# Local attention heads: values as the stationary operand, transposed results, probabilities divided by GpSimd before they are transposed

## The reference, cut to what matters

```python
def swa_sinks_attention(q, k, v, sinks):
    ...
    scores = jnp.einsum('bnqkgd,bnskd->bnkgqs', qb, kb).astype(jnp.float32) * scale
    ...
    sink = sinks.astype(jnp.float32).reshape(1, 1, A_KV_HEADS, A_GROUP, 1, 1)
    m = jnp.maximum(jnp.max(scores, axis=-1, keepdims=True), sink)
    p = jnp.exp(scores - m)
    denom = jnp.sum(p, axis=-1, keepdims=True) + jnp.exp(sink - m)
    p = (p / denom).astype(v.dtype)
    out = jnp.einsum('bnkgqs,bnskd->bnqkgd', p, vb)
...
        mixed = jnp.concatenate([out_a.reshape(b, s, A_Q_W), out_b.reshape(b, s, B_W)], axis=-1)
        x = x + jnp.einsum('bse,ed->bsd', mixed, w_out)
```

## Time and profile before

| what | us |
|---|---|
| median of 3 runs | 2722.82 (2721.86 to 2727.66) |
| the profiled execution | 2724.15 |
| its span in the trace | 2722.3 |
| TensorE busy | 2633.6 (97%) |
| VectorE busy | 1837.4 (67%) |
| ScalarE busy | 1326.2 (49%) |
| GpSimd busy | 405.3 (15%) |
| attention stage, from its first score to the last result | 1742.2 to 1987.6 of the span |

### The profile page before, as it was taken

One profiled execution on the slowest core, in us unless ns is written; L12 is line 12 of the kernel. 1 busy time (PEld: TensorE's weight loads), 2 busy tenths in 40 slices (PEclk: granted clock), 3 DMA queues, 4 the chain that ended last, 5 costly groups with the idle time before them and its releaser, 6 DMA issues. The chain is left out here.

```text
span 2722.3 us, 37072 instructions
## 1 busy us (share of the span) xinstructions
PE 2633.6 (97%) x13612; PEld 2193.7 (81%) x13612; DVE 1837.4 (67%) x2469; ACT 1326.2 (49%) x1952; POOL 405.3 (15%) x359
## 2 busy tenths in 40 slices
PE   8999999999999899999999999899999999999999
PEld 7888876877788888888888788778888788888887
DVE  5761365457524888888888857566625875857878
ACT  3111243567432577877787422555533553525353
POOL 0222212100230122222221022300020000000000
PEclk9999999999999999999999999999999999999999
DMA  3115124311452699999999332100032616253451
GB/s 128 54 47 182 40 74 131 127 39 52 137 179 109 237 378 380 386 381 371 374 371 348 139 105 68 39 1 1 1 132 66 266 49 248 71 187 135 157 183 62
DMA packets 142456, 437.83 MB, mean 161 GB/s; under 512 B 23408, under 2 KB 45680, under 8 KB 110576
## 3 DMA queue, kind: packets, MB, share of 16 engines
q1 hardware_dynamic: 125312, 402.40, 41.0%
q0 software_dynamic: 10656, 20.99, 2.2%
q10 hardware_dynamic: 6352, 12.58, 1.2%
HBM read 387.68 MB, written 66.06 MB: 167 GB/s over the span
## 5 line engine op out<-in xcount | busy, mean ns | idle before, releaser
L2729 DVE TENSOR_TENSOR w_lo<-w_raw,w_hi 128x2048 fp32r<-128x2048 f32 x192 | 437.2, 2293 | 60.3 <-ACT w_hi L2663 59.3
L2663 ACT ACTIVATE w_hi<-w_raw 128x2048 fp32r<-128x2048 f32 x187 | 355.8, 1925 | 39.5 <-PE banks L2790 39.5
L3660 PE MATMUL banks<-b_parts,a_parts 128*128 128x512 f32 x1344 | 306.9, 390 | 6.3 <-DVE a_parts L3715 6.3
L3660 PE MATMUL banks<-a_parts,b_parts 128*128 128x512 f32 x1344 | 306.0, 389 | 2.3 <-DVE a_parts L3715 1.2
L3660 PEld LDWEIGHTS banks<-b_parts,a_parts 128*128 128x128 f32 x1344 | 251.8, 188 | 60.9 <-DVE a_parts L3715 8.8
L3660 PEld LDWEIGHTS banks<-a_parts,b_parts 128*128 128x128 f32 x1344 | 252.0, 188 | 55.2 <-DVE a_parts L3715 1.6
L3689 ACT ACTIVATE b_parts<-w_quarter 128x1024 fp32r<-128x1024 f32 x112 | 118.6, 1059 | 281.4 <-PE banks L3660 266.8
L766 POOL TENSOR_TENSOR w_lo<-w_raw,w_hi 128x512 fp32r<-128x512 f32 (+2 forms) x132 | 158.6, 1207 | 576.6 <-ACT w_hi L745 575.4
L745 ACT ACTIVATE w_hi<-w_raw 128x512 fp32r<-128x512 f32 (+2 forms) x132 | 73.9, 573 | 324.0 <-PE banks L824 306.0
L3709 DVE TENSOR_TENSOR b_parts<-w_quarter,b_parts 128x1024 fp32r<-128x1024 f32 x112 | 136.9, 1222 | 132.5 <-ACT b_parts L3689 132.5
L824 PE MATMUL banks<-w_hi,act_hi 128*128 128x512 f32 (+1 forms) x576 | 219.9, 382 | 6.0 <-POOL w_lo L766 3.7
(11 more groups left out here) (545 smaller groups left out, 5560.8 us busy)
## 6 DMA issues: line engine op xcount, KB each, us to landing
w_raw<-in_w SPq DMA_DIRECT2D x192, 1024.0 KB, 7.4
a_parts<-scratch_x_parts SPq DMA_DIRECT2D x42, 1024.0 KB, 4.8
w_raw<-in_w_in SPq DMA_DIRECT2D x80, 256.0 KB, 2.7
w_quarter<-in_w_up SPq DMA_DIRECT2D x16, 1024.0 KB, 6.9
w_quarter<-in_w_down SPq DMA_DIRECT2D x16, 1024.0 KB, 8.0
scratch_x_parts<-a_parts SPq DMA_DIRECT2D x14, 1024.0 KB, 5.1
scratch_gateT<-gate_staged SPq DMA_DIRECT2D x32, 256.0 KB, 2.2
gate<-scratch_gateT SPq DMA_DIRECT2D x32, 256.0 KB, 3.6
```

What stands on the lines that cost most here:

```text
L2663: act.activation(hi[c % SLOTS][:, :], raw[c % TILES][:, :], ACT.Copy).then_inc(hi_done, 1)
L2729: dve.tensor_tensor(lo[c % SLOTS][:, :], raw[c % TILES][:, :], hi[c % SLOTS][:, :].bitcast(F32), ALU.subtract).then_inc(lo_done, 1)
L3660: mm = pe.matmul(out, left, right, start=(start and n == 0), stop=(stop and n == 2))
```

## The change

The local units now divide first and weigh with the roles swapped.

- ScalarE makes the sinks' exponential ahead of the four others. VectorE, in iteration p+1 behind the maximum of unit p+1, waits for the exponentials of unit p and forms the inverses two heads at a time (`normalise`). GpSimd then multiplies the probabilities in place, in two instructions of two heads each. `turn(p)` waits for both.
- ScalarE makes rounded high parts of LOW and of HIGH (`a_hi`), and VectorE the low parts of both (`a_lo`). The values are split once per tile into high and low columns of one 128x128 stationary operand (`values`, `split_values`). `weigh` has four matmuls of 512 columns instead of eight float32 products. The result stands transposed in the bank, the high values' part in 64 rows and the low values' part in the other 64. ScalarE moves one part across (`cross`, two instructions), VectorE adds the other (`out`, two instructions).
- Since the local results are already transposed, the output stage transposes only the forgetting half (32 transposes). The new `MixedRows` also interleaves the rounding of weights and rows by hand-written orders, and TensorE waits per row tile (`rows_ready`) instead of for all.
- In the last tile the order of units is three forgetting, local, three forgetting, local, two forgetting.

```diff
         @block.gpsimd
         def _(pool):
-            for t in range(2, NT):
-                pool.wait_ge(scored, starts[t - 1])
-                for step in range(2):
-                    ops.pool_part(pool, t, step)
+            def normalise(p):
+                u, s, q = units[p], p % 4, probs[:, p % 3, :]
+                for a in (0, 2):
+                    pool.wait_ge(inverted, 2 * windows_upto[p] + a // 2 + 1)
+                    own, c = slice(a, a + 2), slice(a * u.keys, (a + 2) * u.keys)
+                    x = q[:, c].rearrange("p (a k) -> p a k", a=2)
+                    pool.tensor_tensor(x, x, inv[:, s, own].unsqueeze(2).broadcast_to([P, 2, u.keys]), ALU.mult).then_inc(normed, 1)
+
+            for p in range(n_units):
+                if is_window(p - 1):
+                    normalise(p - 1)
+                if prepares(p) and prepares(p)[1] < 2:
+                    pool.wait_ge(scored, starts[prepares(p)[0] - 1])
+                    pool.wait_ge(normed, 2 * windows_upto[p])
+                    ops.pool_part(pool, *prepares(p))
+                    pool.wait_ge(ops.prep_pool, ops.dve_upto[prepares(p)])
...
+            def normalise(p):
+                s = p % 4
+                for a in (0, 2):
+                    dve.wait_ge(exped, exped_upto[p] + 1 + a + 2)
+                    own = slice(a, a + 2)
+                    then(dve.tensor_tensor(inv[:, s, own], sums[:, s, own], snk[:, s, own], ALU.add))
+                    dve.reciprocal(inv[:, s, own], inv[:, s, own]).then_inc(inverted, 1)
...
             def turn(p):
                 u = units[p]
+                if u.window:
+                    pe.wait_ge(normed, 2 * windows_upto[p + 1])
+                    free_banks(p - 1)
+                    for b in range(len(u.key_tiles)):
+                        for a in range(HALF):
+                            c = a * u.keys + b * P
+                            mm = pe.transpose((LOW, HIGH)[b][:, a * P:(a + 1) * P], probs[:, p % 3, c:c + P], v.ident[:, :])
+                        mm.then_inc((turned_low, turned_high)[b], 1)
+                    return
...
+                if u.window:
+                    pe.wait_ge(values_split, u.i + 1)
+                    for b, j in enumerate(u.key_tiles):
+                        vals = values[:, j, u.g * P:(u.g + 1) * P]
+                        pe.matmul(v.bank[6 + p % 2][:, :], vals, aT_hi(p, b), start=(b == 0), stop=False)
+                        mm = pe.matmul(v.bank[6 + p % 2][:, :], vals, a_lo[:, b, :], start=False, stop=(j == u.i))
+                    mm.then_inc(weighed, 1)
+                    return
...
+class MixedRows:
+
+    BY_POOL = (3, 6)
+    ACT_ORDER = ("b0", "a0", "b1", "a1", "w0", "b2", "a2", "b3", "a3", "b4", "a4", "w1", "b5", "a5", "b6", "a6", "b7", "a7", "w2", "w3")
+    POOL_ORDER = ("w0", "a3", "w1", "a6", "w2", "w3")
```

More of the change, by code:

```diff
@@ L813, in _ @@
                         pe.wait_ge(free, freed[b])
+                    for s, count in tile.rows_ready.get(u, ()):
+                        pe.wait_ge(s, count)
                     if tile.kind == "nat":
@@ L3250, in __init__ @@
         self.width, self.exps = self.keys * (AH // AKV), AH // AKV + 1
-        first = max(0, i - 1)
-        self.blocks = [(a * self.keys + (j - first) * P, j, a, j == first, j == i) for a in range(AH // AKV) for j in range(first, i + 1)]
+        self.key_tiles = list(range(max(0, i - 1), i + 1))
 def attention2_stage(v):
@@ L3304, in attention2_stage, with is_window, aT_hi, by_side @@
     weighed, weigh_read = sem("weighed"), sem("weigh_read")
+    inverted = sem("inverted")
+    normed, values_split, hi_turned, crossed = sem("normed"), sem("values_split"), sem("hi_turned"), sem("crossed")
+    windows_upto = np.cumsum([0] + [u.window for u in units]).tolist()
+    hi_upto = np.cumsum([0] + [len(u.key_tiles) if u.window else 0 for u in units]).tolist()
+    splits_values = {0: 0, **{windows_at[t] - 1: t for t in range(1, NT)}}
+    def is_window(p):
+        return 0 <= p < n_units and units[p].window
+    def aT_hi(p, b):
+        return a_hi[:, p % 2, b * N:(b + 1) * N]
+    def by_side(x, r, side):
+        return x[r, :].rearrange("p (m e q) -> p m e q", m=2, e=2)[:, :, side, :]
+    def own_heads(u, r):
+        c = 2 * u.g * P
+        return v.out_aT[r, u.i, c:c + 2 * P].rearrange("p (m q) -> p m q", m=2)
+    SIDES = (slice(0, HD), slice(HD, P))
     def prepares(p):
@@ L3320, in turn_out, with cross @@
                     act.wait_ge(weighed, p - 1)
+                if units[p].window:
+                    for b in range(len(units[p].key_tiles)):
+                        if b:
+                            act.wait_ge(turned_high, high_upto[p + 1])
+                        act.activation(aT_hi(p, b), (LOW, HIGH)[b], ACT.Copy).then_inc(hi_turned, 1)
+                    return
                 c = min(units[p].width, N)
                 act.activation(aT[:, p % 2, :c], LOW[:, :c], ACT.Copy).then_inc(low_read, 1)
+            def cross(p):
+                u = units[p]
+                act.wait_ge(weighed, p + 1)
+                for side in range(2):
+                    act.activation(own_heads(u, SIDES[side]), by_side(v.bank[6 + p % 2], SIDES[1 - side], side), ACT.Copy).then_inc(crossed, 1)
             for p, u in enumerate(units):
@@ L3358, in turn_out @@
             def turn_out(p):
+                if units[p].window:
+                    if p >= 2:
+                        dve.wait_ge(weighed, p - 1)
+                    for b in range(len(units[p].key_tiles)):
+                        dve.wait_ge(hi_turned, hi_upto[p] + b + 1)
+                        dve.tensor_tensor(a_lo[:, b, :], (LOW, HIGH)[b], aT_hi(p, b).bitcast(F32), ALU.subtract).then_inc((low_read, high_read)[b], 1)
+                    return
                 if halves[p] < 2:
@@ L3370, in out @@
                 if u.window:
-                    then(dve.tensor_tensor(inv[:, s, :], sums[:, s, :], snk[:, s, :], ALU.add))
-                    then(dve.reciprocal(inv[:, s, :], inv[:, s, :]))
-                    c = u.g * HALF * HD
-                    dve.tensor_tensor(v.out_a[:, u.i, c:c + HALF * HD].rearrange("p (a d) -> p a d", d=HD),
-                                      v.bank[6 + p % 2].rearrange("p (a g d) -> p a g d", g=AKV, d=HD)[:, :, u.g, :],
-                                      inv[:, s, :].unsqueeze(2).broadcast_to([P, HALF, HD]), ALU.mult).then_inc(weigh_read, 1)
+                    dve.wait_ge(crossed, 2 * windows_upto[p + 1])
+                    for side in range(2):
+                        made = own_heads(u, SIDES[side])
+                        (dve.tensor_tensor(made, by_side(v.bank[6 + p % 2], SIDES[side], side), made, ALU.add)
+                         .then_inc(*((weigh_read, 1) if side else (link_a, 1))))
                 else:
@@ L3411, in _ @@
                     ops.dve_part(dve, *prepares(p), (LOW, HIGH))
[L3412 removed]
+                if p >= 3 and not is_window(p - 3):
                     out(p - 3)
+                if p in splits_values:
+                    split_values(splits_values[p])
             turn_out(n_units - 2)
@@ L3512, in output2_stage, with load_w @@
     ready, free, x_in = sem("bank_ready"), sem("bank_free"), sem("x_in")
-    prelude = turn_rows(v, mixers)
+    ring = Ring(v)
+    mixed = MixedRows(v, ring)
+    tiles[0].rows_ready = {t: mixed.row_waits(t) for t in range(NT)}
+    def load_w(sp):
+        ring.load_first(sp, tiles)
     def load_x(sp):
```

151 lines of the change are left out of this document (86 added, 65 removed).

## The result

The changed kernel takes **2737.18 us** (median of 5 runs, 2735.45 to 2739.5), the kernel before 2722.82 us (5 runs, 2721.86 to 2727.66). The ratio is 1.0049, 95% interval 1.0035 to 1.0064: slower by 14 us. The profiled execution took 2737.18 us with a span of 2735.2.

A forecast was written before the change was run, and what follows sets the result against it. TensorE, busy 2633.6 of 2722.3 us, was taken as the bound. Terms -11.7, +16.9, +5.0, +1.0, -0.3, -6.2, +4.5 summed to +9.2, from the median 2732.0, taken as 2731; own range 2727 to 2737, whole range 2716 to 2743.

The forecast's parts named there:

- Weighing: Local units in attention: four 512-column matmuls take 0.92 us instead of 1.70, saving 11.7 us in all.
- GpSimd's division: Local units in attention: TensorE's transposes wait for GpSimd's multiplications, twelve units late, +16.9 us.
- Splitting: Preparations behind local transposes: LOW and HIGH come free later through rounding and subtraction, six places, +5.0 us.
- Cover of `kb` preparations: Attention: three preparations of keys lose their cover because the weighing beside them is shorter, +1 us.
- Clock: Attention: TensorE's clock falls behind gaps of 1 to 2 us; three falls of about 1.5 us counted, +4.5 us.
- Output stage and end: Output stage: first product follows the rows, -6.2 us; end of attention shorter with a forgetting unit last, -0.3 us.
- VectorE and GpSimd would lock each other out: Output stage: if so, rows 6 and 7 come up to 2 us later and the stage gives 4.2.
- GpSimd to fit into the slack: Rival, chance 0.2: at 0.65 us per multiplication, division waits shrink to 3 us; faster, 2713.6 us.
- The draw: Rival, chance 0.25: waits as reckoned, clock does not fall, gaps absorb part of preparations' waits; about 2725 us.
- The rival with ten falls: Rival, chance 0.1: the clock falls at nearly every local unit in attention, +20 us, 2743 us.

The follow-up runs named there:

- e9: Changed kernel with VectorE's two additions for an older local unit's result put after the subtractions that free LOW and HIGH, not before; 2726.92 us.
- e1: Changed kernel without the division of the local probabilities, transposes waiting for the exponentials alone; 2724.65 us.
- e5: Changed kernel with VectorE in GpSimd's place for the division of the local probabilities; 2748.45 us.

## Why the forecast came out near, and where its steps were wrong

2731 us was forecast and 2737.2 measured: slower, inside the range, just beyond the forecast's own range (2727 to 2737). Yet the terms are less good than the sum; a too large wait and a too small clock term cancelled. That the time came out within 6 us of the forecast is luck to that extent. With 0.47 us for each us of slow clock, the 20.0 us of attention in the two profiled executions come apart as follows: idle time +17.6, clock +12.9 (27.3 us more), and as the remainder TensorE's work at the higher level, -10.5.

- **Weighing: -11.7 forecast, -10.5 as that remainder.** Read directly, the matmuls stand 0.23 us apart, as forecast, but the second comes 0.32 us behind the first, so a unit's weighing takes 1.01 us up to the next start and not 0.92:

```profile
1971.84 0.48 PE L3508 MATMUL banks<-a_hi,values 128*128 128x512 f32 x1
1972.16 0.40 PE L3509 MATMUL banks<-a_lo,values 128*128 128x512 f32 x1
...
1972.85 1.89 PE L3463 MATMUL banks<-kaT,qaT 128*128 128x256 f32 x8
```

  Against 1.71 before that is 0.70 us in 14 units and 0.27 in the two of tile 0, 10.3 us. Right, and a little too large.
- **GpSimd's division: +16.9 forecast, +6.9 measured.** The step that failed first. GpSimd's multiplication takes 1.04 us, not the 1.24 of the subtraction from which I priced it:

```profile
L3334 POOL TENSOR_TENSOR probs<-probs,inv x32: 612/1039/1042, 1747.0 to 1996.5; 128x512 f32<-128x512 f32 x28, 128x256 f32<-128x256 f32 x4
```

  That is 0.4 us for each of the twelve places, 4.8 us; it is worked out, no run changed it. In six of the 16 units 0.3 us of it was lost again, since VectorE's second addition was held up beside GpSimd's first half (last section). From the first addition to TensorE's start the chain takes 2.6 us, and 2.9 in such a unit, where I had 3.2 from a point just ahead of the addition. The number of places was the other half: TensorE waited in six of them. In tiles 4 to 6 the waits are 1.24, 1.31, 1.05, 0.72 and 0.41 (forecast 1.8, 1.9, 1.6, 1.65, 1.3), in tile 7 none, in tile 0 2.16 (forecast 1.4). In tile 1 GpSimd was done at 1773.03, but TensorE came to the transposes at 1776.64: a preparation ahead of them had waited 2.61 us. Waits in a row hide each other, and I had added them up. In tile 6 the second local unit was to be 1.35 us late; there GpSimd was done at 1966.25, and TensorE came at 1967.60. The new order of the last tile puts the preparation (at 1964.04) ahead of this unit's transposes, where it had stood behind them, and I had taken the timeline of the kernel before for it.
- **Splitting: +5.0 forecast, +8.8 measured.** The number, six, is right, and so nearly is the size of the three in later tiles (1.05 against 0.9). The three in tiles 0 and 1 were 1.42, 2.37 and 1.89, where I had given two places 0.7 each. What I overlooked is VectorE's order: its additions for an older unit ahead of the subtraction, which e9 shows for the 2.37.
- **Cover of `kb` preparations: +1 forecast, +2.0 measured.** Small, right in kind.
- **Clock: +4.5 forecast, +12.9 measured.** The mechanism was right, the size almost three times too small. The price was right for what it was read from: a stretch of 3.4 us at the lower level costs 1.6 us at 0.47, where eight slow dense matmuls had given me 1.5. I counted three falls more; there are four more (six stretches instead of two), and three of the six last 10.2, 6.8 and 6.8 us instead of 3.4. So it is their length that I had missed. The number can't be had by counting gaps either, since with e9 2 us of idle time took 24 us of slow clock along. All kernels here with more idle time than before have more slow clock, but not in proportion.
- **Output stage and end: -6.5 forecast, -7.3 measured.** Right in its size. The forecast had no clock in it: the kernel before has 6.8 us of the lower level in this stretch, the changed one none. How much of the 7.3 us that is was not tested; e9, with the same stage and 3.4 us of it, needs 14.2 us against 14.0, so it is little once rows and weights set the pace. That VectorE and GpSimd would lock each other out was left to the bounds. The low parts of local rows took VectorE 0.92 and 0.98 us where GpSimd ran beside them, and 0.68 alone, while one of the other halves' subtractions, which read one input from the banks, took 0.69 beside GpSimd too (at 2016.48). The product waited only 0.9 us in all for its rows. So the lock is there and cost little.

The rivals: for GpSimd to fit into the slack its half had to be below 0.85 us; 1.04 lies half way to my 1.24, and the gain would have been lost to `a_lo` and the clock all the same (e1, with no division at all, only comes back to the kernel before). The draw needed a clock that doesn't fall. The rival with ten falls, 20 us, was about as far from the clock's 12.9 on one side as my forecast was on the other.

What stays open: why the clock falls behind one gap and not behind an equal one. The Trainium skill, "TensorE: Matmul & The Clock Gate", section "What's actually happening", says that the chip's look at the engine's activity runs freely and does not start anew with the kernel, and that the point at which the clock changes varies for that reason. By it the same gap can fall differently. The pair of equal gaps above agrees with it, and so does the spread of 10 us over eleven runs; no run here moves a gap on purpose to prove it. Nor was it tried to have the low part made by another engine than VectorE.

## What to carry to other kernels

Where TensorE stands in a pipeline two units deep, what counts is not how much work an engine gets but what it makes first: turning round two steps of VectorE (10.3 us, 2 of them idle time and most of the rest the clock) and letting the transposes start with the first half of their data (4.0 us) gave more than taking the division to a faster engine, which lost 11. Read at each gap what the releasing engine did between the moment its input was ready and the moment it began. And put a price on short gaps beyond their length: each us at the lower clock cost 0.47 us here, and how many of them a gap brings varies from run to run and from place to place, so the range has to hold it.

## What the hardware showed that I had not expected

**VectorE and GpSimd lock each other out, and it is seen on an instruction of 0.15 us.** The first addition of two columns takes 0.15 us, the second, which starts while GpSimd multiplies, 0.69, and it ends with the multiplication:

```profile
1879.26 0.15 DVE L3388 TENSOR_TENSOR inv<-sums,snk 128x2 f32<-128x2 f32 x1
...
1879.76 1.04 POOL L3334 TENSOR_TENSOR probs<-probs,inv 128x512 f32<-128x512 f32 x1 [7.76 <-DVE inv L3389]
...
1880.12 0.69 DVE L3388 TENSOR_TENSOR inv<-sums,snk 128x2 f32<-128x2 f32 x1 [0.51 <-ACT probs L3309]
...
1881.09 1.04 POOL L3334 TENSOR_TENSOR probs<-probs,inv 128x512 f32<-128x512 f32 x1 [0.29 <-DVE inv L3389]
```

So GpSimd's second half starts 0.29 us late, because its own first half had held up the inverse for it; the same 0.29 or 0.30 us stand in six of the 16 local units. The Trainium skill states the rule in "SBUF — State Buffer", section "Who interferes with whom": a VectorE instruction with two SBUF inputs contends with a GpSimd one that reads SBUF. The trace agrees, 0.69 against 0.15 us.

**GpSimd multiplies faster than it subtracts with rounding.** 1.04 us for 128x512 with one input repeated along the columns, 1.29 for the subtraction that writes rounded numbers (a form with other inputs and another output type, so what makes the difference isn't shown). VectorE's 0.69 for the same multiplication (e5) makes it 1.5 times as fast. The Trainium skill's rule of keeping two-input work on VectorE ("GPSIMD Engine Reference", section "Engine selection"), which gives GpSimd as about twice as slow, would have chosen worse here: 2748.45 against 2737.18 us, with 1.5 measured for this multiplication.
